# One-hots of the first dense tile on GpSimd, and sixteen more row products beside the fourth tile's search

## What is computed

```
t1, i1 = top_k(s1, 16); t2, i2 = top_k(s2, 16)          # two half keys of 128
top, pos = top_k(t1 (+) t2, 16)                         # the 16 best pairs of a head
idx = the experts' numbers;  g = softmax(top)
a = einsum('thkd,td->thk', u_tab[idx], x)               # 128 dot products a token
w = gelu(a) * g
out = einsum('thk,thkd->td', w, v_tab[idx])             # 128 rows of v, weighted
```

## Time and profile before

| | |
|---|---|
| median of 3 runs | 3737.01 us (3734.82 to 3744.37) |
| span of the profiled execution | 3731.3 us |
| profiled execution, time of its own | not given apart from its span |
| PE busy | 3458.3 us, 93% |
| DVE busy | 2778.5 us, 74% |
| POOL busy | 1616.2 us, 43% |
| ACT busy | 862.9 us, 23% |
| moved by DMA | 1263.48 MB, mean 339 GB/s |

### The profile page before, as it was taken

One profiled execution on the slowest core, in us unless ns is written; L12 is line 12 of the kernel. 1 busy time (PEld: TensorE's weight loads), 2 busy tenths in 40 slices (PEclk: granted clock), 3 DMA queues, 4 the chain that ended last, 5 costly groups with the idle time before them and its releaser, 6 DMA issues.

```text
span 3731.3 us, 38289 instructions
## 1 busy us (share of the span) xinstructions
PE 3458.3 (93%) x12478; PEld 2108.1 (56%) x12478; DVE 2778.5 (74%) x6049; ACT 862.9 (23%) x2206; POOL 1616.2 (43%) x1362
## 2 busy tenths in 40 slices
PE   6898999999889999999988988999897989999998
PEld 2555446888677344444435554488786854444443
DVE  0488787999788866666646887789987897666667
ACT  1116211148632000000021260111675210000000
POOL 2044275423641555555400552634256326455552
PEclk9898999999899999999989989999998999999999
DMA  9966588989999999999974865899899989999995
GB/s 356 330 232 225 180 328 339 360 293 326 409 406 366 358 399 413 414 414 413 376 265 154 310 206 185 327 349 388 275 366 408 399 319 390 414 413 413 412 413 202
DMA packets 413989, 1263.48 MB, mean 339 GB/s; under 512 B 36240, under 2 KB 139664, under 8 KB 370784
## 3 DMA queue, kind: packets, MB, share of 16 engines
q0 software_dynamic: 192000, 721.61, 50.0%
q1 hardware_dynamic: 171808, 514.19, 36.6%
q10 hardware_dynamic: 49984, 25.23, 2.2%
HBM read 1174.06 MB, written 86.84 MB: 338 GB/s over the span
## 4 chain that ended last, share of the span: by engine, by line
PE 40%; DMA 29%; DVE 17%; issue 6%; POOL 5%; ACT 1%; SPq 1%; ACTq 0%; DVEq 0%; POOLq 0%
DMA ring<-in_peer_v_dram,eidx 14%; PE P L940 12%; DMA ring<-in_peer_u_dram,eidx 10%; PE P L914 7%; POOL ring L679 5%; PE T L952 4%; DVE late L1319 4%; PE P L748 4%; PE P L765 4%; DMA ring<-in_w_mod_dram 2%; DVE ring L1301 2%; PE O L812 2%; PE T L748 2%; DMA gate_d<-area 1%; PE P L801 1%
## 5 line engine op out<-in xcount | busy, mean ns | idle before, releaser
L679 POOL DMA_INDIRECT ring<-in_peer_u_dram,eidx x768 | 949.6, 1237 | 1147.2 <-DVE ring L1301 764.3
L1301 DVE SCALAR_TENSOR_TENSOR ring<-ring,h 128x1024 f32<-128x1024 f32 x768 | 925.4, 1223 | 294.3 <-DMA ring<-in_peer_u_dram,eidx 286.3
L968 PE MATMUL P<-w_ring,area 128*128 128x512 f32 x2048 | 934.3, 600 | 38.5 <-DVE area L1475 37.1
L679 POOL DMA_INDIRECT ring<-in_peer_v_dram,eidx x512 | 626.8, 1224 | 694.9 <-DVE late L1319 376.9
L940 PE MATMUL P<-hT,w_ring 128*128 128x256 f32 x4096 | 925.8, 385 | 0.0
L940 PEld LDWEIGHTS P<-hT,w_ring 128*128 128x128 f32 x4096 | 782.4, 194 | 104.1
L968 PEld LDWEIGHTS P<-w_ring,area 128*128 128x128 f32 x2048 | 391.2, 192 | 544.3 <-issue 544.3
L1319 DVE SCALAR_TENSOR_TENSOR h<-ring,dots,h 128x1024 f32<-128x1024 f32 x254 | 325.8, 1283 | 182.9 <-DMA ring<-in_peer_v_dram,eidx 174.5
L1319 DVE SCALAR_TENSOR_TENSOR late<-ring,dots,late 128x1024 f32<-128x1024 f32 x254 | 325.7, 1282 | 53.8 <-DMA ring<-in_peer_v_dram,eidx 38.2
L914 PE MATMUL P<-hT,w_ring 128*128 128x128 f32 (+1 forms) x1024 | 286.0, 441 | 2.9 <-issue 2.9
L968 PE MATMUL O<-w_ring,qT 128*128 128x512 f32 x512 | 261.4, 592 | 0.0
(11 more groups left out here) (227 smaller groups left out, 3292.7 us busy)
## 6 DMA issues: line engine op xcount, KB each, us to landing
w_ring<-in_peer_uT_dram SPq DMA_DIRECT2D x128, 1024.0 KB, 7.9
w_ring<-in_peer_vB_dram SPq DMA_DIRECT2D x128, 1024.0 KB, 8.0
ring<-in_w_mod_dram POOLq DMA_DIRECT2D x48, 1024.0 KB, 8.3
w_ring<-in_peer_wq_dram SPq DMA_DIRECT2D x64, 512.0 KB, 5.8
h<-acts_d SPq DMA_DIRECT2D x64, 512.0 KB, 9.0
w_ring<-in_w_in_dram SPq DMA_DIRECT2D x48, 512.0 KB, 4.8
area<-gate_d SPq DMA_DIRECT2D x16, 1536.0 KB, 14.1
hT<-gate_d SPq DMA_DIRECT2D x16, 1536.0 KB, 14.6
```

Source lines behind the costliest of these rows:

```text
L679: pool.indirect_dma_start(out=ring[:, b, :], out_offset=None, in_=tables["uv".index(phase)], in_offset=bass.IndirectOffsetOnAxis(ap=eidx[: ...
L968: mm = pe.matmul(bank[ACC[2 * t + half]][:, :], w, uv_ring[:, b // 2 % (WR // 2), b % 2, half * 512:(half + 1) * 512], start=b == 0, stop= ...
L1301: dve.scalar_tensor_tensor(ring[:, b, :], ring[:, b, :], 1.0, h2[:, k, :], ALU.mult, ALU.mult, accum_out=dots[:, k, row:row + 1]).then_inc ...
```

## The change

GpSimd makes tile 3's one-hots that were DVE's: four TENSOR_SCALAR of 128 elements for the second one-hots of a quad, one for the first. ScalarE's three stay. Quad q is made right before the gather of u row `hots_row(q)` of tile 1 and has a semaphore of its own, `pool_hots`, on which PE's g job waits. DVE drops tile 3's quads and does 32 rows beside the search of tile 4 (16 to 47) instead of 16, rows 48 to 57 behind it, and 70 rows instead of 78 in the stage of tile 4.

```diff
+HOTS_ASIDE = 3
+ROWS_BESIDE = 32
...
+def hots_row(q):
+    if q < SEARCH_CHUNKS:
+        return 16 + GP + ROWS_BESIDE * q // SEARCH_CHUNKS
+    return 16 + GP + ROWS_BESIDE + q - SEARCH_CHUNKS
...
+                def one_hots(q):
+                    if q == 0:
+                        pool.wait_ge(emptied["O"], emptied_at(("slT", HOTS_ASIDE), l))
+                    if q >= OH_BUFS:
+                        old = ("g", HOTS_ASIDE, q - OH_BUFS)
+                        pool.wait_ge(full[BANK[old]], full_at(old, l))
+                    for j in range(QUAD):
+                        t = q * QUAD + j
+                        pool.tensor_scalar(oh_b[q % OH_BUFS][:, j, :], iota128, slotT[:, 1, t:t + 1], None, ALU.is_equal)
+                    for j in range(ACT_SIDE, QUAD):
+                        t = q * QUAD + j
+                        ins = pool.tensor_scalar(oh_a[q % OH_BUFS][:, j, :], iota128, slotT[:, 0, t:t + 1],
+                                                 slotT[:, 2, t:t + 1], ALU.is_equal, ALU.mult)
+                    ins.then_inc(pool_hots, 1)
...
                     for r in range(lo, hi):
+                        if (phase, k) == ("u", 1):
+                            for q in range(CHUNKS):
+                                if hots_row(q) == r:
+                                    one_hots(q)
...
-                        pe.wait_ge(oh_ready, l * (len(V_DENSE) * CHUNKS) + n + 1)
+                        if k == HOTS_ASIDE:
+                            pe.wait_ge(pool_hots, l * CHUNKS + job[2] + 1)
+                        else:
+                            pe.wait_ge(oh_ready, l * (2 * CHUNKS) + n - CHUNKS + 1)
...
                 for i in range(2 * PH + 6):
-                    dot_rows(1, 16 + 16 * i // 22, 16 + 16 * (i + 1) // 22)
-                    one_hots(3, i)
+                    dot_rows(1, 16 + ROWS_BESIDE * i // 22, 16 + ROWS_BESIDE * (i + 1) // 22)
                     choosing(4, i)
                 slots_out(4)
-                for i in range(CHUNKS - SEARCH_CHUNKS):
-                    one_hots(3, SEARCH_CHUNKS + i)
-                    dot_rows(1, 32 + i, 33 + i)
-                dot_rows(1, 42, 50)
+                near = 16 + ROWS_BESIDE + CHUNKS - SEARCH_CHUNKS
+                dot_rows(1, 16 + ROWS_BESIDE, near)
                 for i in range(CHUNKS):
                     one_hots(4, i)
-                    dot_rows(1, 50 + 78 * i // CHUNKS, 50 + 78 * (i + 1) // CHUNKS)
+                    dot_rows(1, near + (SLOTS - near) * i // CHUNKS, near + (SLOTS - near) * (i + 1) // CHUNKS)
```

More of the change, by code:

```diff
@@ L446, in build @@
         oh_ready = sem("oh_ready")
+        pool_hots = sem("pool_hots")
         oha_far = sem("oha_far")
```

## The result

| | before | after |
|---|---|---|
| median | 3740.05 us (3734.82 to 3744.37, 4 runs) | 3832.44 us (3825.68 to 3836.55, 4 runs) |
| span of the profiled execution | 3731.3 us | 3831.4 us |

What follows compares the result with a forecast made beforehand. Tile 4's stage was taken as bound by DMA bandwidth. Per layer, +12 us (tail) and -16 us (stage) give -4, two layers -8, set off the 3737.0 us median: 3729 us, range 3701 to 3766.

Steps and rivals of the forecast that it cites:

- part 3's price: GpSimd's one-hots for tile 3: 0.25 us an instruction, 1.25 us a quad; upper end 0.5 and 2.5 us.
- "No loss" in the half-key part: Search of tile 4: a GpSimd quad takes 4.2 us, PE takes one per 4.35 us, so PE loses nothing.
- The tail: Between the search's end and tile 4's slT: quad 31 ready 12 us late, so tile 4's stage starts 12 us late.
- each waits behind a product: Quad 23 after the search: each of its five GpSimd instructions waits behind a DVE row product, 5 x 1.4 = 7 us.
- Rival 2: GpSimd's rate becomes the bound: 0.5 us an instruction, quads 28 us late, 12 us a layer lost, 3761 us; chance 0.23.
- threshold of 0.33 us: GpSimd's price per one-hot instruction from which the tail's loss reaches the 16 us gained in tile 4's stage.
- Part 2: Tile 4's stage, with 70 rows instead of 78 and DVE early, gets 16 us shorter, to about 141 us.
- Part 1: Sixteen rows more beside tile 4's search fit the DMA: 83 GB/s on 275 makes 358, under 408.
- Rival 3: Bandwidth only moved: stores hold PE in the search, the stage's gain is spent, 3737 to 3743 us; chance 0.1.
- The search keeps its length: Tile 4's search stays at 101 us but for port waits, as 18.4 us of rows replace 18.9 of quads on DVE.
- the 105 that I had named as a sign: A search of tile 4 longer than 105 us on DVE would break the claim that sixteen more rows fit there.
- The signs named for "wrong": GpSimd instructions of 0.4 us or more in DVE's free time, PE waiting already in the search; no slT wait; 150 us stage.

Runs made afterwards that it cites:

- the run with every second quad: Changed kernel, but GpSimd makes only tile 3's quads 0, 2, .. 30 and VectorE the others; 27 rows beside the search, 69 in the stage: 3755.92 us.
- both helpers: Changed kernel with GpSimd on quads 0, 2, .. 14 only, ScalarE making the fourth weighted one-hot of odd quads below 16; 25 rows beside the search: 3743.76 us.
- one of five instructions: Changed kernel without GpSimd's four compares a quad, only the weighted one-hot left, buffers cleared at the start; tile 3's gates not computed: 3724.3 us.

## Why the prediction was wrong

- **The failed step is part 3's price.** I took 0.25 us from the select and called twice DVE's 0.26 the upper end. Measured: 0.607 us for a compare, 0.783 for the weighted one, above even that end. 160 instructions are 103 us a layer, not 40. Neither row bounded it. The select has the same size on the same engine and lacks the operand per token, but a compare with a constant still takes 0.528 us, so it is not the operand that makes the difference. And twice VectorE's 0.26 was the price of another engine for the weighted one, which takes three times as long here. The Trainium skill ("GPSIMD Engine Reference", section "4.1 Engine selection") has one-input work at roughly line rate there, the half that I followed; the trace does not agree: 0.783 us against VectorE's 0.26 for the weighted one-hot, and 4 x 0.607 against 0.60 for a quad's compares.
- **"No loss" in the half-key part** fell with it. I had 4.2 us a quad; it was 6.2 (130.2 us from quad 0 to quad 21, over 21). By its parts: 3.2 of one-hots, 2.0 of gathers (1.45 a quad at 1.17 and the idle time beside it), 1.0 of waits. Without waits for the port it would be about 5 (3.2 and 1.45 gathers at 1.01 + 0.16), still over 4.35; with the old 0.73 rows a quad it would be 4.1, which is why quads 0 to 10 kept the pitch in the run with rows as before. Loss 38 us, as quad 21 in the changed kernel and with the tail on VectorE show.
- **The tail** was to cost 12 and cost 24. The form was right (single gathers, PE at 2.62 us a quad), and 4.36 us undisturbed was 2.49 in my sum: (4.36 - 2.62) x 10 = 17 us with no wait at all. My "each waits behind a product", 1.4 us, was too low for the worst case (1.9 in the run with every second quad, 3.0 where one alone is held), but in the changed kernel DVE ran out of rows and most of the tail went unheld.
- **Rival 2 is what happened**, with its sign and its mechanism (PE waits in the search already, from quad 3) and 0.23 of the chance. Its size, 28 us late, was 62 a layer, mainly because it too had 0.5 us: with 3.2 us a quad its own sum gives some 50. Its threshold of 0.33 us holds up in an estimate from the measured rows: from quad 0 to 31 POOL may take 115 us and its start of 7; 42 gathers take 58 with the idle time, so 160 instructions have 0.40 us each, waits included, and with 0.16 of waits (26 us over 160) the price may be 0.24 before tile 4's slT is late at all. If it may be 16 us late, as much as I gave the stage, the price may be 0.34.
- **Part 2 was right**: 139.2 and 140.9 us against "about 141", and its reason too: DVE waited 35.9 us with a full ring, and only 34.4 MB of rows came in the stage, 65.7 rows, where 70 were used. It was worth 19 and I had 16. But this gain goes with DVE being early: where DVE came on time, 4 to 6 rows fewer gave under 5 us and 9 fewer (both helpers) 1.0 and 3.8 us; where it waited for the slT and its ring filled (35.9 us in the changed kernel, 22.5 with one of five instructions) 70 rows for 78 gave 19 and 20. For the rows alone DVE waited 11.6 us, PE's slT was 19 us late and the stage as much shorter, no gain at all. My sum had counted it as a gain next to a tail that was late; the lateness was part of its reason. No run has DVE early with all 78 rows, so how the 19 us divide between fewer rows and a full ring is open.
- **Part 1 was right** on bandwidth. Rival 3 fell by its mechanism, as neither rows nor loads were waited for in the first stretch with the rows alone; the time of that run, 3739.78, lies within the rival's 3737 to 3743 and would not have decided. "The search keeps its length" was wrong (121 us, over the 105 that I had named as a sign) for a reason not in it: DVE waited 18.8 us there for rows that POOL issued late.
- The signs named for "wrong" (0.4 us or more in DVE's free time, PE waiting in the search already) were the ones that came.

## What to carry to other kernels

Before work goes to an engine that is idle, price one instruction of exactly that kind on exactly that engine: a row of another engine is no bound, and it takes one run with a single such instruction to learn the price. Then compare paces, not shares: GpSimd was at 43% of the span, and the question was whether a quad there takes less than the 4.35 us in which PE uses one. And work in a gathering engine's queue is paid twice when it is late, once by who waits for it and once by who waits for the gathers behind it.

## What I had not expected of the hardware

- GpSimd's TENSOR_SCALAR, by two sizes: 2.6 ns an element and 0.28 us fixed for 128 partitions in f32; 0.08 us for a scalar per token; 0.18 us for the second operation with its scalar (0.783 less 0.607). Its select of the same size takes 0.28 us in all.
- Behind VectorE's products in a row a GpSimd instruction of 0.78 us lasted up to 3.71 us, while the longest product of layer 0 beside such instructions took 1.58 us instead of 1.22, 0.36 more. So GpSimd waited through whole products, and no product waited through a whole instruction of GpSimd's.
- After waits of about 4 us PE's next quad took 2.04 and 2.05 us instead of 1.13 (in layer 1 one took 1.30 behind 4.00). The same matmuls took 20 us more in the first stretch, time in which PE would otherwise have waited for POOL.
